# Weight units of a two-block kernel loaded by two transfers (120 and 8 partitions) instead of one of 128

## The chip, the cores and the metric

The program runs on one core of one Trainium2 chip. The metric is the time of one execution on the device in microseconds (us), of which the median over several runs is compared.

## The reference, cut to what matters

The input is a sequence of 512 tokens of width 1024 in float32. It passes through two blocks.

The first block normalises the tokens, multiplies them by a weight matrix `w_in`, and takes from the product the inputs of a convolution branch, of a windowed attention branch with 16 heads, and of two sets of gates. The branches are projected, gated, added, projected again by `w_out`, and added to the input. After that comes a feed-forward part over 16,384 experts. A query projection gives scores; for each of the 512 tokens and each of 8 heads the 16 best experts are picked, and the rows of `peer_u` and `peer_v` that belong to them are read:

```python
u = expert_u[expert_idx]
act = gelu(einsum('thkd,td->thk', u, hc))
vv = expert_v[expert_idx]
return einsum('thk,thkd->td', gate * act, vv)
```

These are 512 x 8 x 16 pairs of rows of 2 x 1024 numbers each, 536.9 MB.

The second block normalises again, multiplies by a second `w_in`, and runs three branches (a recurrence over the tokens, a sliding-window attention, a cross attention to a memory of 256 tokens), which are gated, projected and added.

## The kernel before, in words

**Weight units.** All projection weights are laid out on the host as 171 units. One unit is 128 partitions x 1024 float32 numbers, 512 KB, so 4 KB for each partition. They lie in the order of their use: 28 for the first product, 24 that fill other stages, 16 for merging, 16 for the queries of the experts, 8 for the memory, and 79 for the second block. The class `Weights` handles them:

- `load` (L198, on SyncE's queue, SP) sends unit u into slot u % 4 of a ring of four (`weight_ring`). Before it, L197 waits until unit u - 4, which lay in that slot, has been used up (`done`). When the transfer has landed, the semaphore `arrived` of the slot has gone up by 16.
- `high_part` (L206, on ScalarE, ACT) waits for `arrived` and rounds the unit into `weight_high`. It is called by `finished`, which waits until unit u is done and then takes unit u + 2.
- `low_parts` (L223) or `low_part` (L231), on GpSimd (POOL) or for the first units on VectorE (DVE), subtract the rounded part from the unit and write the rest over it.
- TensorE (PE) multiplies with three products for each tile (L155 to L157): high x high, high x low, low x high. The last of a unit's 24 matmuls raises `done`.

So the load of unit u + 4 is issued when unit u is done, and its rounding starts when unit u + 2 is done: a load has the time of two units.

**What else is on SyncE's queue.** It works in order. In most stages `load` calls alternate with stores of finished tiles to HBM (`z_store`, L303), with reads of them (`merge_z`, L951 and L2802), and, in the experts' stage, with stores of the scores (`score_store`, L1180) and their reads (`peer_sc`, L1175). At the start SyncE issues x and the constants (L825) and then the first four units.

**The experts' stage.** GpSimd issues 512 indirect gathers (L1349). Each reads one expert for each of 128 tokens, 1 MB in rows of 8 KB, into one of ten slots of `peer_uv`. VectorE multiplies and sums the first half of each row with the token (L1548), ScalarE applies gelu (L1309) and builds diagonal matrices (L1314), and TensorE adds the second halves with them (L1655). The last matmul of two gathers frees their slots. The last units of the query weights and the eight of the memory are loaded, rounded and used beside the gathers; the loads stand at L1178 and L1191.

Of the kernel before, what the change touches and what calls it, by code (L numbers as in the profile page):

```python
# [27 lines left out]
P = 128  # L28
# [7 lines left out]
RING = 4  # L36
# [46 lines left out]
def offsets(widths):  # L83
    at, out = 0, {}
    for name, w in widths.items():
        out[name] = (at, at + w)
        at += w
    return out, at


class Columns:


    def __init__(self, tensor, widths):
        self.tensor, (self.at, self.width) = tensor, offsets(widths)
# [36 lines left out]
def placed(nc, ctx, name, shape):  # L132

    tensor = ctx.enter_context(nc.sbuf_tensor(name, shape, F32))
    return tensor, nc.sbuf_base - 4 * int(np.prod(shape[1:]))


def same_place(nc, name, shape, offset):


    return nc.alloc_sbuf_tensor_at(name, shape, F32, offset=offset)
# [18 lines left out]
class Weights:  # L160
# [2 lines left out]

    def __init__(self, nc, ctx, dram):
        self.nc, self.dram = nc, dram
        self.ring, offset = placed(nc, ctx, "weight_ring", [P, RING, DT, P])
        self.low = same_place(nc, "weight_low", [P, RING, DT, P], offset)
        self.high, self.high_offset = placed(nc, ctx, "weight_high", [P, 2, DT, P])  # L170
        self.arrived = [ctx.enter_context(nc.semaphore(f"weights_arrived{s}")) for s in range(RING)]
        self.high_ready = ctx.enter_context(nc.semaphore("weights_high_ready"))
        self.split = ctx.enter_context(nc.semaphore("weights_split"))
        self.done = ctx.enter_context(nc.semaphore("unit_done"))
        self.issued = self.highs = self.lows = 0
# [15 lines left out]
    def load(self, sp, upto):  # L191

        upto = max(min(upto, TOTAL), self.issued)

        def one(u, i):
            if u >= RING:
                sp.wait_ge(self.done, RING * i + (u - RING + 1))  # L197
            sp.dma_start(self.ring[:, u % RING], self.dram[u + RING * i]).then_inc(self.arrived[u % RING], 16)  # L198
        self.units(sp, self.issued, upto, one)
        self.issued = upto  # L200

    def high_part(self, act, u, i=0):

        if u < TOTAL:
            act.wait_ge(self.arrived[u % RING], 16 * i + 16 * (u // RING + 1))
            self.nc.scalar.activation(self.high[:, u % 2].bitcast(F32R), self.ring[:, u % RING], ACT.Copy  # L206
                                      ).then_inc(self.high_ready, 1)
            self.highs = u + 1
# [2804 lines left out]
```

## Time and profile before

| | us |
|---|---|
| median of 3 runs | 2619.27 (2618.55 to 2622.28) |
| the profiled execution, its own time | 2615.85 |
| its span, first to last instruction | 2614.0 |
| around the span | 1.85 |
| TensorE busy | 2224.1 (85%) |
| VectorE busy | 1661.2 (64%) |
| ScalarE busy | 872.3 (33%) |
| GpSimd busy | 853.1 (33%) |
| mean rate of the 16 DMA engines | 261 GB/s |

The profile is of one execution. It cuts the span into 40 equal slices of 65.35 us; a digit is the busy share of an engine in that slice, in tenths. The shares are averages over stages that have different limits, so each stage has to be read by itself.

### The profile page before, as it was taken

Reading aid. Unit: us, or ns where it says so; the run is one execution under the profiler, and the core shown is the slowest. Engines: PE = TensorE matmul, PEld = TensorE weight load, DVE = VectorE, ACT = ScalarE, POOL = GpSimd, SP = SyncE. Lnnn points to the kernel's source line nnn. Section 1 sums busy time; section 2 is a strip of 40 time slices with the busy share of each in tenths; the row PEclk is TensorE's granted clock in tenths of the full one; section 3 lists DMA queues with packets and bytes.
Section 4 is the critical chain, followed back from the end, with each engine's and each line's share of the span. In section 5 each row is a group of like instructions: output and inputs, shape, how many; then the busy total and the mean of one; then the engine's idle time right before and its main releaser. Section 6 shows DMA issues by size and latency. Waiting matters only on the chain. (4 is left out here: it accounts for less than half of the span.)

```text
span 2614.0 us, 33173 instructions
## 1 busy us (share of the span) xinstructions
PE 2224.1 (85%) x11846; PEld 1388.6 (53%) x11846; DVE 1661.2 (64%) x3847; ACT 872.3 (33%) x1939; POOL 853.1 (33%) x649
## 2 busy tenths in 40 slices
PE   8998999889987888777777777777788999989999
PEld 7886667765543333322222222322266788766787
DVE  7998797257776777766776667766403533546443
ACT  3222762333323242322322223222233322235531
POOL 0001213355443455444433343333232212112243
PEclk9999999999999999999999999999989999979999
DMA  4332215289999999999999999999722222332253
GB/s 152 105 109 85 84 51 177 73 301 419 421 422 419 421 420 419 420 418 416 416 420 416 417 407 420 413 415 416 312 89 74 73 71 68 104 113 86 89 189 105
DMA packets 131073, 682.46 MB, mean 261 GB/s; under 512 B 13536, under 2 KB 23136, under 8 KB 65120
## 3 DMA queue, kind: packets, MB, share of 16 engines
q0 software_dynamic: 73728, 536.90, 49.7%
q1 hardware_dynamic: 57184, 143.47, 16.0%
q8 instruction: 94, 1.54, 0.2%
q14 instruction: 67, 0.55, 0.1%
HBM read 655.68 MB, written 24.64 MB: 260 GB/s over the span
## 5 line engine op out<-in xcount | busy, mean ns | idle before, releaser
L1655 PE MATMUL bank<-peer_uv,peer_diag 128*128 128x512 f32 x2048 | 959.6, 613 | 299.2 <-ACT peer_diag L1314 292.4
L1548 DVE SCALAR_TENSOR_TENSOR peer_uv<-peer_uv,early_h 128x1024 f32<-128x1024 f32 x512 | 639.5, 1260 | 389.4 <-DMA peer_uv<-in_peer_uv,peer_index 389.4
L1655 PEld LDWEIGHTS bank<-peer_uv,peer_diag 128*128 128x128 f32 x2048 | 379.3, 194 | 841.4 <-issue 838.4
L1349 POOL DMA_INDIRECT peer_uv<-in_peer_uv,peer_index x512 | 524.0, 1024 | 753.6 <-PE bank L1655 665.0
L223 POOL TENSOR_TENSOR weight_low<-weight_ring,weight_high 128x1024 fp32r<-128x1024 f32 x102 | 249.0, 2442 | 703.5 <-ACT weight_high L206 703.5
L155 PE MATMUL bank<-hT_high,weight_high 128*128 128x512 f32 x952 | 404.3, 425 | 16.9 <-PEq L1675 3.9
L157 PE MATMUL bank<-hT_high,weight_low 128*128 128x512 f32 x952 | 375.4, 394 | 0.0
L156 PE MATMUL bank<-hT_low,weight_high 128*128 128x512 f32 x952 | 375.1, 394 | 0.0
L206 ACT ACTIVATE weight_high<-weight_ring 128x1024 fp32r<-128x1024 f32 x171 | 180.7, 1057 | 468.3 <-PE bank L157 448.1
L1309 ACT ACTIVATE peer_gelu<-peer_dots 128x2 f32<-128x2 f32 x256 | 52.1, 203 | 801.9 <-DVE peer_uv L1548 801.9
L155 PEld LDWEIGHTS bank<-hT_high,weight_high 128*128 128x128 f32 x952 | 182.0, 191 | 72.7 <-issue 20.8
L1314 ACT ACTIVATE peer_diag<-const,peer_weight 128x128 f32<-128x128 f32 x512 | 177.5, 393 | 114.6 <-DVE peer_weight L1453 109.6
L156 PEld LDWEIGHTS bank<-hT_low,weight_high 128*128 128x128 f32 x952 | 181.9, 191 | 44.1 <-issue 10.7
L157 PEld LDWEIGHTS bank<-hT_high,weight_low 128*128 128x128 f32 x952 | 181.0, 190 | 39.5
L231 POOL TENSOR_TENSOR weight_low<-weight_ring,weight_high 128x1024 fp32r<-128x1024 f32 x29 | 79.5, 2743 | 291.5 <-ACT weight_high L206 291.1
L868 DVE SCALAR_TENSOR_TENSOR convT_whole<-z_u,cols,convT_whole 128x512 f32<-128x512 f32 x120 | 89.2, 743 | 0.0
L868 DVE SCALAR_TENSOR_TENSOR z_odd<-z_u,cols,z_odd 128x512 f32<-128x512 f32 x112 | 83.2, 743 | 0.0
L1453 DVE SCALAR_TENSOR_TENSOR peer_weight<-peer_gelu,peer_r,peer_e 128x2 f32<-128x2 f32 x256 | 54.5, 213 | 39.7 <-ACT peer_gelu L1309 39.7
L470 DVE SCALAR_TENSOR_TENSOR attn_logit<-const,bank 128x256 f32<-128x256 f32 (+2 forms) x96 | 39.2, 449 | 44.8 <-PE bank L415 44.5
L494 DVE TENSOR_SCALAR attn_prob<-attn_prob,attn_recip 128x256 f32<-128x256 f32 (+2 forms) x112 | 63.0, 598 | 0.1
L231 DVE TENSOR_TENSOR weight_low<-weight_ring,weight_high 128x1024 fp32r<-128x1024 f32 x40 | 48.7, 1217 | 10.1 <-ACT weight_high L206 10.1
L1309 ACT ACT_TABLE_LOAD x40 | 51.3, 1283 | 0.7
(410 smaller groups left out, 2696.8 us busy)
## 6 DMA issues: line engine op xcount, KB each, us to landing
weight_ring<-in_weights SPq DMA_DIRECT2D x171, 512.0 KB, 3.7
z_store<-fill_stage SPq DMA_DIRECT2D x70, 256.0 KB, 2.4
peer_uv<-in_peer_uv,peer_index POOLq DMA_INDIRECT x512
merge_z<-z_store SPq DMA_DIRECT2D x8, 768.0 KB, 6.2
merge_z<-z_store SPq DMA_DIRECT2D x12, 512.0 KB, 5.0
score_store<-peer_work SPq DMA_DIRECT2D x16, 192.0 KB, 11.6
peer_sc<-score_store SPq DMA_DIRECT2D x24, 128.0 KB
swz<-z_store SPq DMA_DIRECT2D x1, 2560.0 KB, 11.2
```

Of the source, the lines that this page charges most:

```text
L155: nc.tensor.matmul(to, left[0], right[0], start=start, stop=False)
L156: nc.tensor.matmul(to, left[0], right[1], start=False, stop=False)
L157: return nc.tensor.matmul(to, left[1], right[0], start=False, stop=stop)
L206: self.nc.scalar.activation(self.high[:, u % 2].bitcast(F32R), self.ring[:, u % RING], ACT.Copy).then_inc(self.high_ready, 1)
L223: self.nc.gpsimd.tensor_tensor(self.low[:, slot].bitcast(F32R), self.ring[:, slot], self.high[:, u % 2], ALU.subtract).then_inc(self.split, 1)
L231: vector.tensor_tensor(self.low[:, u % RING].bitcast(F32R), self.ring[:, u % RING], self.high[:, u % 2], ALU.subtract).then_inc(self.split, 1)
L868: nc.vector.scalar_tensor_tensor(to, u[:, c, k:k + T], cols("conv_w", k * DT + c), to, ALU.mult, ALU.add).then_inc(tap_done, 1)
L1309: nc.scalar.activation(gelu[:, at], dots[:, at], ACT.Gelu).then_inc(gelu_done, 1)
L1314: nc.scalar.activation(diag[:, p % SLOTS], ident, ACT.Copy, scale=weight[:, p % TOPK:p % TOPK + 1]).then_inc(diag_ready, 1)
L1349: pool.indirect_dma_start(uv[:, p % SLOTS], None, peer_uv, bass.IndirectOffsetOnAxis(index[:, n % 2, p % TOPK:p % TOPK + 1], 0)).then_inc( ...
L1548: nc.vector.scalar_tensor_tensor(uv[:, p % SLOTS, 0:D], uv[:, p % SLOTS, 0:D], 1.0, h2[:, t], ALU.mult, ALU.mult, accum_out=dots[:, p % TO ...
L1655: mm = nc.tensor.matmul(bank[2 * (t % 2) + c][:], diag[:, p % SLOTS], uv[:, p % SLOTS, D + c * 512:D + (c + 1) * 512], start=(p % PICKS == ...
```

## The change

Each unit is sent by two transfers on the same queue, one after the other: partitions 0 to 119, then 120 to 127. Each of them raises the slot's semaphore by 16, so the waiting side counts in steps of 32. Bytes, slots, order, and all other instructions are the same.

```diff
+    MOST = 120
...
         def one(u, i):
             if u >= RING:
                 sp.wait_ge(self.done, RING * i + (u - RING + 1))
-            sp.dma_start(self.ring[:, u % RING], self.dram[u + RING * i]).then_inc(self.arrived[u % RING], 16)
+            for rows in (slice(0, self.MOST), slice(self.MOST, P)):
+                sp.dma_start(self.ring[rows, u % RING], self.dram[u + RING * i][rows]).then_inc(self.arrived[u % RING], 16)
...
         if u < TOTAL:
-            act.wait_ge(self.arrived[u % RING], 16 * i + 16 * (u // RING + 1))
+            act.wait_ge(self.arrived[u % RING], 32 * i + 32 * (u // RING + 1))
```

## Rows read from the trace of the kernel before

**Rows 1.** The page's 40 slices: busy tenths by engine, DMA share, GB/s.

```profile
PE   8998999889987888777777777777788999989999
DVE  7998797257776777766776667766403533546443
DMA  4332215289999999999999999999722222332253
GB/s 152 105 109 85 84 51 177 73 301 419 421 422 419 421 420 419 420 418 416 416 420 416 417 407 420 413 415 416 312 89 74 73 71 68 104 113 86 89 189 105
```

**Rows 2.** Stretches: engine busy us (instructions), granted TensorE clock, DMA share, GB/s.

```profile
440.00:500.00 60.00, 56.83 (x244) 45.41 (x242) 22.92 (x33) 16.87 (x23) 24.55 (x10) 1.00 0.30 99
...
1200.00:1400.00 200.00, 149.17 (x326) 59.34 (x326) 139.16 (x383) 59.00 (x155) 79.83 (x79) 0.98 1.01 417
```

**Rows 3.** Waits over the whole span, us in total, times, longest.

```profile
POOL peer_uv L1349 <- PE bank L1655: 665.0, 244, 6.5
...
DVE peer_uv L1548 <- DMA peer_uv<-in_peer_uv,peer_index: 389.4, 235, 9.7
...
ACT weight_high L206 <- DMA weight_ring<-in_weights: 11.9, 2, 8.0
```

**Rows 4.** All 171 loads (L198): SyncE's issue time in ns, and us to landing.

```profile
L198 SPq DMA_DIRECT2D weight_ring<-in_weights x171: 327/332/992, 3.6 to 2587.5; - x171
...
DMA to landing us min/median/max: 3.4/3.7/15.6
```

**Rows 5.** ScalarE's timeline while units follow each other: start, us, instruction, idle before.

```profile
440.87 1.06 ACT L206 ACTIVATE weight_high<-weight_ring 128x1024 fp32r<-128x1024 f32 x1 [4.54 <-PE bank L157]
446.47 1.06 ACT L206 ACTIVATE weight_high<-weight_ring 128x1024 fp32r<-128x1024 f32 x1 [4.54 <-PE bank L157]
```

**Rows 6.** The waits of SyncE's own queue.

```profile
SPq L198 <- PE bank L157: 952.4, 147, 97.9
```

**Rows 7.** ScalarE's timeline where the gathers begin.

```profile
558.35 1.06 ACT L206 ACTIVATE weight_high<-weight_ring 128x1024 fp32r<-128x1024 f32 x1 [8.02 <-DMA weight_ring<-in_weights]
...
564.46 1.06 ACT L206 ACTIVATE weight_high<-weight_ring 128x1024 fp32r<-128x1024 f32 x1 [3.91 <-DMA weight_ring<-in_weights]
...
567.96 0.20 ACT L1309 ACTIVATE peer_gelu<-peer_dots 128x2 f32<-128x2 f32 x1
```

**Rows 8.** The loads issued beside the gathers, from 560 us on.

```profile
L198 SPq DMA_DIRECT2D weight_ring<-in_weights x18: 327/458/496, 560.8 to 1058.0; - x18
...
DMA to landing us min/median/max: 5.2/9.1/15.5
```

**Rows 9.** DMA queues by packets, MB and share of 16 engines, 1200 to 1400 us.

```profile
q0 software_dynamic: 11348, 82.65, 100.1%
```

**Rows 10.** The same, 106 to 109.6 us: one load lands alone.

```profile
DMA packets 144, 0.52 MB, mean 146 GB/s; under 512 B 16, under 2 KB 16, under 8 KB 144
...
q1 hardware_dynamic: 144, 0.52, 44.6%
```

**Rows 11.** Three stretches of 20 us in which the gathers run below their rate (columns as in rows 2).

```profile
1540.00:1560.00 20.00, 15.54 (x35) 5.93 (x33) 14.06 (x42) 6.26 (x15) 8.19 (x8) 1.00 0.98 384
1240.00:1260.00 20.00, 16.14 (x32) 6.42 (x32) 13.92 (x38) 3.79 (x13) 8.80 (x9) 0.91 1.00 405
1640.00:1660.00 20.00, 15.47 (x32) 6.05 (x31) 13.45 (x35) 5.11 (x18) 8.66 (x8) 0.91 1.00 400
```

**Rows 12.** The first load, issued at 3.56 us.

```profile
DMA to landing us min/median/max: 8.3/8.3/8.3
```

**Rows 13.** ScalarE's timeline where it takes the first unit.

```profile
12.50 0.20 ACT L767 ACTIVATE z_rms<-z_ms 128x1 f32<-128x1 f32 x1 [1.08 <-DVE z_ms L837]
12.61 1.04 ACT L206 ACTIVATE weight_high<-weight_ring 128x1024 fp32r<-128x1024 f32 x1
```

## Prediction

> **What bounds the kernel now.** I read the slices first, since this kernel has stages with different limits [rows 1]. From about 560 to 1880 us the DMA digit is 9 and the rate stands at 413 to 422 GB/s in nearly all slices, while TensorE falls to 7 or 8 and VectorE to 6 or 7. Before and after that TensorE is at 8 or 9 and the DMA engines at 1 to 5. So there are two regimes, and the change, which touches only DMA transfers, has to be priced in each.
>
> Then come two stretches [rows 2]. In the first TensorE is busy 56.83 of 60 us and the DMA share is 0.30: TensorE is the bound. In the second TensorE is busy 149 of 200 us and the DMA share is 1.01: the gathers are the bound. The waits say the same [rows 3]. VectorE waited 389.4 us for gathered rows, in 235 places. GpSimd's wait of 665.0 us for TensorE is for free slots; it costs nothing as long as the engines have gathers queued, and a share of 1.0 says that they have.
>
> The weight loads themselves stand in the list of waits once: ScalarE waited for a load twice, 11.9 us together [rows 3]. All other 169 found their unit landed.
>
> **The change, part by part.**
>
> *Issue on SyncE.* There are 171 more DMA instructions. One takes a median of 0.33 us [rows 4], up to 0.49 beside the gathers [rows 8], so SyncE is occupied for some 57 to 84 us more. None of it should reach the end: at the loads SyncE sits waiting for TensorE for 952.4 us, in 147 of the 171 cases [rows 6]. What stands behind a load in this queue (the tile stores, the reads for merging, the score stores) is delayed by 0.33 to 0.49 us each. Nobody waits for a tile store; the readers prefetch two tiles ahead. I cost this at nothing. Its cover is that slack; without it the cost would be 0.33 us for each of some 40 loads that a read or a score store follows, 13 us.
>
> *Landing in the TensorE stages.* A load lands 3.7 us after issue [rows 4]. Units follow each other in 5.60 us (446.47 - 440.87, [rows 5]), and a load has two units, 11.2 us. 7.5 us are spare. The second issue adds 0.33 us, and one more packet on some engine about 0.2 us: 128 packets of 4 KB took 44.6% of 16 x 3.6 us, 0.20 us each [rows 10]. Even if all 8 rows of the small transfer went through one engine, 8 x 0.20 = 1.6 us would fit. About 150 of the loads lie there: cost 0. The first unit lands at 3.56 + 8.3 = 11.9 us [rows 12] and is taken at 12.61, with no wait on the load, right behind the step at 12.50 [rows 13]. One packet more still fits into these 0.7 us: 0.
>
> *Bytes beside the gathers.* Here the engines have no idle time, so every microsecond that a load takes from the busiest engine is paid. Eighteen loads are issued from 560 us on [rows 8], and the one for which ScalarE waits until 564.46 [rows 7] was issued before them: 19. The packets of a gather give the price: 82.65 MB in 100.1% of 16 x 200 us is 0.0388 us per KB, so 0.16 us for a row of 4 KB and 0.32 for one of 8 KB [rows 9]. Before, one transfer is 128 packets of 4 KB and 16 small ones [rows 10], which I read as eight rows for each of 16 engines and an end mark from each. After, 120 rows can't be even (7.5 each), and 8 rows are sent apart. The trace of before shows no such transfer, so I bound it. Low end: the busiest engine still carries 8 rows, 0 us. High end: the busiest ones carry 16, 8 x 0.16 x 19 = 24 us. I take 9 rows, the full eight of the large transfer plus one of the small, since eight is what each engine carries today: 19 x 0.16 = **3.0 us**.
>
> By the Trainium skill, "DMA: Bandwidth & Descriptors", section "Why a DMA increments its semaphore by 16 and not by 1", a transfer uses the largest number of engines up to 16 that divides its rows, from the lowest-numbered on: 15 for 120 rows, 8 for 8. Eight engines would carry nine rows, seven eight and one none, and by that the sum would be the same 3.0 us; no row here shows it.
>
> *The handover to the gathers.* The two loads for which ScalarE waits end at 558.35 and 564.46 us; gelu of the first gathers starts only behind them, at 567.96 [rows 7]. Between two packets of a load an engine sends one of a gather, so one row more comes 0.16 + 0.32 = 0.5 us later. The second wait ends by its own load, so the two don't add: **0.5 us**, with 0 and 3.8 us (eight rows) as ends.
>
> *Given back.* A lag of a few engines is lost again where the gathers run below their rate for another reason. Against 421 GB/s, three stretches of 20 us miss (1 - 384/421) x 20 = 1.8, 0.8 and 1.0 us [rows 11], and all come after the last load at 1058 us. There the engines that aren't behind idle a little longer and the others catch up. They need not be the same waits; I take **-1 us**, with 0 and -3.5 as ends.
>
> The sum is 3.0 + 0.5 - 1.0 = **+2.5 us**. On the profiled execution that is a span of 2616.5 and a time of 2618.4 us. It lay 3.4 us below the median of the runs, so against the median of 2619.3 I forecast **2621.8 us**. That is +0.1%, less than the 0.2% (5.2 us) that a measurement of this kernel can tell from no change.
>
> **The rivals.**
>
> *A. Wholly hidden, 2619 us.* The busiest engine gets no more than today, or the lag is all caught up in the dips. For it: some 3.6 us of dips [rows 11] can cover 3.5. Against it: they are short, and a share of 0.98 to 1.00 in them means that most engines are still busy.
>
> *B. Slower by over 0.2%: the gathers lose more than a row per load.* The place is the stretch from the handover to 1066 us, where 19 loads share saturated engines. If each costs r packets of 4 KB instead of one, because its rows are divided unevenly or because two engines then write to the same part of SBUF and hold each other up, the price is r x 3.0 + 0.5 us. From r = 2 it passes 5.2 us. At r = 4, half of the eight rows, it is +12.5, 2631.8 us; at r = 8, with 3.8 us at the handover, +27.8, 2647 us. For it: a gather's pace is that of the slowest engine, and these stages have no spare share [rows 2]. Against it: ten gathers are in flight, so engines can take turns in lagging.
>
> By the Trainium skill, "SBUF — State Buffer", section "Door 1: The DMA port swizzle", four neighbouring partitions share a port, the next four lie on another, and 32 further it is the same port again. If the 15 engines take eight neighbouring rows each, engine and port no longer match one to one as in the transfer of 128; that is the second cause in B. No row here shows ports.
>
> *C. Faster: one engine paces the gathers, and it is relieved.* If one engine that is slower than the rest gets no row of the loads any more, it saves up to 8 x 0.16 x 19 = 24 us, but no more than its distance from the next slowest. Against it: an engine that all others wait for would leave them idle, and the share is 1.01 [rows 2], 100.1% for the gathers' queue alone [rows 9]. What is left is under 1% of 500 us, 5 us; I give it -6 us, 2613. The Trainium skill, "DMA: Bandwidth & Descriptors", section "Latency and other measured facts", says that engines 7 and 15 are usually slower in traces, which is what would make this case; it names two, and relieving one of them leaves the other.
>
> *D. The large transfer uses only a few engines.* With one engine it would take 120 x 0.2 = 24 us, over twice the 11.2 us that it has; the TensorE stages would be bound by it, some 13 us for each of 150 units, a time over 4000 us. Nothing in the trace points to it, and nothing excludes it but that 120 divides well.
>
> **How the numbers follow.** Forecast 0.47, A 0.20, B 0.26, C 0.06, D 0.01. The forecast's own bounds run from +0 to about +6 us: with the scatter of the median I put 0.05 of its 0.47 above +5.2. Faster by over 0.2%: C, 0.06. Slower: B, D and that 0.05, 0.32. Within: 0.62. The range must leave out 0.2 at most: the lower end takes in A and most of C with the 0.1% scatter of the runs, 2614; the upper end takes in B up to r = 4 or 5, 2634. Outside are r above 5, D and the rest of C, together some 0.17.
>
> **What would show each step right or wrong.** The small packets of a load, 16 now, tell how many engines it uses: 23 would be 15 and 8. The loads become 342 issues, with SyncE's medians near 0.33 us, and TensorE's busy time stays near 2224 us. The landing of the loads in the quiet stages stays below 5 us; over 11 us would be D. ScalarE's waits for loads stay two, near 8.5 and 4 us; a third means that cover is gone. The step between the handover and the end of the gathers, 560 to 1893 us, grows by 2 to 3 us, all of it before 1066 us (the last load's issue and landing); growth by 6 or more there is B, and packets of the weight loads then take clearly more than 0.16 us each. A stretch that shrinks there is C. Growth anywhere else proves the forecast wrong in its first two steps.

## The result and the profile after

| | before | after |
|---|---|---|
| median us | 2618.91 | 2655.99 |
| range of four runs | 2615.91 to 2622.28 | 2652.69 to 2659.00 |
| profiled execution, own time | 2615.85 | 2656.61 |
| its span | 2614.0 | 2654.8 |

The change makes the kernel slower by 37.1 us: the ratio is 1.0151, with a 95% interval of 1.0139 to 1.0163. The forecast was +2.5 us and the range ended at 2634. Both were wrong.

The DMA share and the rate of after in 40 slices, against [rows 1] (a slice is 66.4 us now):

```profile
DMA  5433316289999999999999999999922222332373
GB/s 150 107 104 83 84 53 179 75 299 391 384 390 412 420 377 379 390 414 415 421 415 418 420 413 416 411 419 415 384 76 75 83 58 69 91 124 84 87 193 105
```

The DMA digit is 9 in the experts' stage as before. The rate is not as before: 391, 384 and 390 GB/s in three slices, then 412 and 420, then 377, 379 and 390, and from there on 411 to 421 until the slice in which the gathers end. The two valleys are where weight units are loaded, eight in each (before, they were issued from 596 to 760 us and from 905 to 1058 us). Between and after them the gathers run at the rate of before.

Stretches of after (engine busy us and instructions, granted clock, DMA share, GB/s):

```profile
600.00:800.00 200.00, 175.28 (x523) 93.53 (x521) 137.61 (x326) 58.69 (x151) 95.06 (x78) 0.97 1.02 386
800.00:930.00 130.00, 95.68 (x225) 39.87 (x224) 89.50 (x242) 39.69 (x103) 49.31 (x50) 0.99 1.02 420
930.00:1100.00 170.00, 138.33 (x323) 64.73 (x321) 104.07 (x283) 54.55 (x128) 77.73 (x64) 0.89 1.01 382
1200.00:1400.00 200.00, 154.97 (x322) 62.02 (x323) 138.51 (x383) 59.51 (x157) 80.84 (x78) 0.94 1.01 417
```

and the same of before:

```profile
600.00:800.00 200.00, 179.43 (x526) 94.22 (x525) 142.84 (x344) 63.77 (x163) 97.66 (x83) 0.99 1.02 421
800.00:905.00 105.00, 81.97 (x193) 34.38 (x192) 76.54 (x210) 32.59 (x87) 41.28 (x41) 0.98 1.01 421
905.00:1066.00 161.00, 134.22 (x333) 62.72 (x331) 112.89 (x291) 57.52 (x139) 83.08 (x68) 0.96 1.02 419
```

Beside the loads the rate fell from 421 to 386 and from 419 to 382, (1 - 386/421) x 200 = 16.6 and (1 - 382/419) x 170 = 15.0 us. The DMA share stayed 1.01 to 1.02. Behind the loads it was 417 again, as in [rows 2]. So the engines were as busy as before and moved less: a busy share of 1 says that packets are in flight, not that they are fast.

The first and the last gather on GpSimd's timeline, before and then after:

```profile
540.07 1.09 POOL L1349 DMA_INDIRECT peer_uv<-in_peer_uv,peer_index  x1 [2.70 <-DVE peer_index L1435]
1870.30 0.94 POOL L1349 DMA_INDIRECT peer_uv<-in_peer_uv,peer_index  x1 [0.30 <-issue]
```

```profile
543.26 1.09 POOL L1352 DMA_INDIRECT peer_uv<-in_peer_uv,peer_index  x1 [2.71 <-DVE peer_index L1438]
1911.26 0.94 POOL L1352 DMA_INDIRECT peer_uv<-in_peer_uv,peer_index  x1 [0.30 <-issue]
```

Of the 40.8 us between the two spans, 3.2 are there before the first gather, 37.8 come between the first and the last (40.96 - 3.19), and nothing is added behind. What precedes the gathers was expected to be free. It starts with ScalarE taking the first unit late, against [rows 13]:

```profile
13.79 1.06 ACT L209 ACTIVATE weight_high<-weight_ring 128x1024 fp32r<-128x1024 f32 x1 [0.59 <-DMA weight_ring<-in_weights]
```

That is 1.2 us: 0.5 were there one instruction earlier (`z_rms` starts at 13.00 instead of 12.50), and 0.59 are a wait for the load. Most of the rest comes between 240 and 300 us, where the granted clock of TensorE was 0.89 in this profile and 0.94 in that of before: GpSimd's first `weight_low` starts at 238.2 instead of 237.5 us, and the one at 292.5 starts at 295.6. The first experiments below show whether these 3.2 us belong to the change.

The handover, against [rows 7]:

```profile
562.40 1.06 ACT L209 ACTIVATE weight_high<-weight_ring 128x1024 fp32r<-128x1024 f32 x1 [8.88 <-PE bank L157]
...
571.89 1.06 ACT L209 ACTIVATE weight_high<-weight_ring 128x1024 fp32r<-128x1024 f32 x1 [7.30 <-DMA weight_ring<-in_weights]
```

The second unit is taken 571.89 - 564.46 = 7.4 us later, of which 3.2 were there already: the handover cost 4.2 us.

Last, the loads alone. One load in a window of 5 us without gathers, DMA queues by packets, MB and share of 16 engines, before:

```profile
DMA packets 144, 0.52 MB, mean 105 GB/s; under 512 B 16, under 2 KB 16, under 8 KB 144
...
q1 hardware_dynamic: 144, 0.52, 32.1%
```

and after:

```profile
DMA packets 151, 0.52 MB, mean 105 GB/s; under 512 B 23, under 2 KB 23, under 8 KB 151
...
q1 hardware_dynamic: 151, 0.52, 39.5%
```

The 23 small packets, one end mark for each engine by the prediction's reading, fit 15 and 8 engines. That agrees with the rule in the Trainium skill, "DMA: Bandwidth & Descriptors", section "Why a DMA increments its semaphore by 16 and not by 1"; the count alone doesn't exclude another pair with this sum. The share tells more: the same 128 rows occupy engines for 0.395 x 16 x 5 = 31.6 us instead of 25.7, with nothing else beside them. Single loads scatter: for the one in 95 to 100 us it is 36.8% against 33.7%, 29.4 against 27.0 us. Over all loads before the gathers, 0 to 530 us, the difference is clear. SyncE's queue before, after, and for three other ways of sending a unit that the experiments below introduce (112 + 16 partitions, 64 + 64 partitions, two halves of the columns):

```profile
q1 hardware_dynamic: 19008, 54.96, 30.5%
q1 hardware_dynamic: 19503, 54.93, 37.3%
q1 hardware_dynamic: 20192, 54.96, 33.2%
q1 hardware_dynamic: 20165, 54.92, 38.5%
q1 hardware_dynamic: 29664, 54.96, 30.4%
```

The bytes are the same within 0.1% and the packets differ only by end marks, but in the last line by twice the packets as well, and there the share doesn't rise. So it isn't the number of packets or of transfers that makes packets last longer, but the split by partitions, even without gathers.

### The profile page after: what moved, and what is told of

It reads as the page before. It is cut to its first block and busy times, and to the rows that moved or that the text cites. A ratio compares the mean times of both kernels' runs of the same rounds, so it can differ in the third digit from the quotient of the medians.

```text
span 2654.8 us, 33384 instructions
## 1 busy us (share of the span) xinstructions
PE 2241.7 (84%) x11846; PEld 1395.2 (53%) x11846; DVE 1654.9 (62%) x3847; ACT 872.6 (33%) x1939; POOL 853.5 (32%) x649
## 3 DMA queue, kind: packets, MB, share of 16 engines
q1 hardware_dynamic: 58381, 143.48, 18.9%
## 5 line engine op out<-in xcount | busy, mean ns | idle before, releaser
L1658 PE MATMUL bank<-peer_uv,peer_diag 128*128 128x512 f32 x2048 | 976.1, 622 | 319.6 <-ACT peer_diag L1317 310.1
L1658 PEld LDWEIGHTS bank<-peer_uv,peer_diag 128*128 128x128 f32 x2048 | 385.9, 197 | 870.9 <-issue 868.2
L1456 DVE SCALAR_TENSOR_TENSOR peer_weight<-peer_gelu,peer_r,peer_e 128x2 f32<-128x2 f32 x256 | 56.4, 220 | 41.8 <-ACT peer_gelu L1312 41.8
```

The costliest lines, as they stand in the source:

```text
L1658: mm = nc.tensor.matmul(bank[2 * (t % 2) + c][:], diag[:, p % SLOTS], uv[:, p % SLOTS, D + c * 512:D + (c + 1) * 512], start=(p % PICKS == ...
```

## The experiments

Three theories were set against each other. **U**: the cost comes from uneven engines (nine, eight or no rows). **N**: it comes from having two transfers. **P** (place): it comes from which partitions each engine writes, since engines that write to the same part of SBUF at the same time slow each other.

All kernels below differ from before only in a list of pieces that `load` sends one after the other; the waiting side counts the pieces of each slot.

```diff
-            sp.dma_start(self.ring[:, u % RING], self.dram[u + RING * i]).then_inc(self.arrived[u % RING], 16)
+            for to, of in self.pieces(u):
+                sp.dma_start(to(self.ring[:, u % RING]), of(self.dram[u + RING * i])).then_inc(self.arrived[u % RING], 16)
```

"Beside the gathers" means the 20 units `first_unit("query") + 8 <= u < first_unit("query") + 28`: the last eight of the queries, the eight of the memory and the first four of the second block.

**Where the cost lies.** First 120 + 8 for the 20 units beside the gathers only:

```diff
+        cuts = (120, 8) if first_unit("query") + 8 <= u < first_unit("query") + 28 else (128,)
```

> Only the 20 units whose loads are issued from 542 us on, beside the gathers, are sent as 120 + 8 partitions; the other 151 go as one transfer. The cost lies beside the gathers (all theories on how it comes about): +33 to +36 us on before, ratio 1.013, of the +37 of the whole change. If it is the number of transfers on SyncE's queue in general: 20/171 of it, +4 us, 1.002.

Measured: 2653.66 us against 2615.45, +38.2 us, ratio 1.0149 (1.0132 to 1.0166), 2 us above the expected range and in agreement with the +37.1 of the whole change. Then the complement, 151 units split and these 20 whole:

> The complement of the last one: 151 units as 120 + 8, the 20 beside the gathers as one transfer. Cost beside the gathers: only the shifts at the start (+1.2 us) and around 250 us (+2.4) stay, +3 to +4 us, ratio 1.001 to 1.002. If every load costs: +33 us.

Measured: 2615.86 us, +0.4 us, ratio 1.0006 (0.9996 to 1.0015). The whole cost is in the 20 units, 1.9 us for each. The 151 others are free within what can be measured. The expected +3 to +4 us didn't come, so the 3.2 us ahead of the gathers in the profile of after aren't a sure part of the result. The profile of this kernel, which splits the same loads there, also shows ScalarE waiting for the first unit (0.51 us), but its granted clock from 240 to 300 us is 0.94 as before, and its first gather starts at 540.60 us, 0.5 later than before. With columns halved, a kernel that comes below, the clock there is 0.89 again and the first gather starts at 542.05.

**Uneven, two, or place.** An even split in two, by intent 7 rows and 1 row for each engine:

```diff
+        cuts = (112, 16)
```

> All units as 112 + 16 partitions: 7 rows and 1 row for each of 16 engines, 8 rows on each as before, 32 end marks per load. Theory U, uneven load of the engines (nine, eight and no rows): the cost goes, under +5 us, below 1.002. Theory P, place: an engine's rows are no longer those of one part of SBUF that it has to itself, and engines hold each other up; evenness doesn't help: +25 to +45 us, 1.010 to 1.017, and 4 KB packets of the loads take 0.20 us or more beside the gathers. Theory N, two transfers instead of one: as the change, +37 us, with packets at 0.16 us.

Measured: 2644.90 us, +29.5 us, ratio 1.0111 (1.0095 to 1.0128). From 600 to 750 us, 4 KB on SyncE's queue, its other transfers included, took 0.209 us of an engine (10.3% of 16 x 150 us for 4.85 MB), and 0.176 before (9.4% for 5.26): P's sign as well. And an even split in halves:

```diff
+        cuts = (64, 64)
```

> All units as 64 + 64 partitions, 4 rows per engine and transfer, even. U: below 1.002. N: +37 us, 1.014. P: sixteen engines write into one half of SBUF at a time, so they hold each other up at least as much as with 120 + 8: +30 to +60 us, 1.011 to 1.023.

Measured: 2654.55 us, +39.1 us, ratio 1.0149 (1.0132 to 1.0166). Both programs have 59,920 packets on SyncE's queue against 57,184, 16 more for each of 171 loads, which fits 16 end marks for each of the two transfers. U falls with these two: where all 16 engines take part in both transfers and the rows divide evenly, 29 and 39 us are lost. N is still open, and goes with the next, two transfers of all 128 partitions and half the columns each:

```diff
+        return [((lambda t, e=e: t[:, 4 * e:4 * e + 4]), (lambda t, e=e: t[:, 512 * e:512 * e + 512])) for e in range(2)]
```

> All units as two transfers of 128 partitions each, 512 columns (2 KB per row) in each. As many transfers as in the change, but every engine keeps the rows of the single transfer. Theory P (place): the cost goes; only 128 packets more per load, whose 2 KB take 0.084 us instead of 0.080, 0 to +4 us, 1.000 to 1.0015. Theory N (two transfers instead of one): +37 us, 1.014.

Measured: 2618.74 us against 2615.59, +3.2 us, ratio 1.0010 (1.0000 to 1.0019). As many transfers, and twice the packets for each load, cost 3 us, between 0 and 5 by the interval. The rates in 40 slices of the 150 us from 600 on show it best. Before, six loads land here and can't be seen:

```profile
GB/s 425 412 427 419 422 428 417 421 419 427 419 419 417 421 428 419 422 421 411 424 430 424 419 415 425 414 420 431 419 419 426 414 423 430 415 415 419 420 427 417
```

With 120 + 8 each is a hole of two or three slices of 3.75 us:

```profile
GB/s 406 398 281 324 377 422 419 422 425 419 329 289 422 419 422 417 423 338 294 425 422 414 419 362 283 401 422 419 418 419 409 294 345 419 419 424 417 354 280 409
```

With halves of the columns there are none:

```profile
GB/s 417 410 423 424 422 421 421 420 424 412 419 420 421 418 419 418 424 422 417 421 422 418 420 417 419 416 426 425 410 424 422 418 419 424 420 413 417 426 420 415
```

**Place alone.** A pair of kernels that differ in nothing but the place. Both send partitions 64 to 127 of the 20 units in one transfer and 0 to 63 in eight transfers of eight partitions. In the one they are neighbours:

```diff
+        at = [slice(8 * m, 8 * m + 8) for m in range(8)] + [slice(64, P)]
```

> Only the 20 units beside the gathers: partitions 0 to 63 by eight transfers of eight neighbouring partitions, 64 to 127 by one transfer. The busiest engines carry 12 rows: U alone gives +4 x 0.16 x 20 = +13 us. P: the eight engines of a small transfer write next to each other and take turns, up to 4 rows one after the other: 0.48 us lost for each of 8 x 20 small transfers, +77 us, with the large one's +20 and the unevenness +60 to +110 us, 1.023 to 1.042.

Measured: 2692.73 us, +77.1 us, ratio 1.0294 (1.0277 to 1.0311). In the other each transfer takes every fourth partition of 32:

```diff
+        at = [slice(32 * h + a, 32 * h + 32, 4) for h in range(2) for a in range(4)] + [slice(64, P)]
```

> The same with partitions 0 to 63 by eight transfers of every fourth partition, so that engine j gets the rows of the four-partition group that it has in the single transfer too. Same number of transfers, same bytes and rows per engine as with neighbouring partitions; only the place differs. P: +15 to +35 us (half of 64 + 64's loss, and the unevenness), at least 30 us less than with neighbours. U and N: the same time as with neighbours within 5 us.

Measured: 2654.65 us, +39.1 us, ratio 1.0147 (1.0130 to 1.0164). The same transfers, bytes and packets: both programs have 58,464 packets on SyncE's queue, 64 more than before for each of 20 loads, which is eight end marks for each small transfer. Neighbours cost 38.1 us more, 0.24 us for each of 160 small transfers. The +39 of the spread one is above the +35 that was given as its highest value: half of 64 + 64's loss (20) and the unevenness (13) make 33, and 6 us are unexplained. The DMA queues of the two, 600 to 750 us, neighbours first:

```profile
q0 software_dynamic: 6941, 50.56, 90.9%
q1 hardware_dynamic: 3597, 4.38, 9.8%
```

```profile
q0 software_dynamic: 7190, 52.35, 90.6%
q1 hardware_dynamic: 3792, 4.85, 10.1%
```

The gathers' queue (q0) holds the engines for the same share in both, and moves 50.56 against 52.35 MB in it. It moved 57.80 before. The gathers' own packets slow down; it isn't only that the loads take longer.

This pair changes the place in SBUF and in HBM at once. The next two part them. In the first the small transfers write neighbouring partitions (`NEAR`, the first list of slices) and read every fourth row (`FAR`, the second), in the other the reverse:

```diff
-        return [((lambda t, s=s: t[s]), (lambda t, s=s: t[s])) for s in at]
+        return [((lambda t, s=s: t[s]), (lambda t, r=r: t[r])) for s, r in zip(NEAR, FAR)]
```

> The pair of eights changed two places at once: where the rows lie in SBUF and where in HBM. Here the small transfers write eight neighbouring partitions and read every fourth row of HBM; so the weights of these 20 units come in a wrong order of rows, and the output is another. If the place in SBUF is what counts: the time with neighbours, +72 to +82 us, 1.0275 to 1.0315. If the place in HBM counts: the time with spread rows, +34 to +44 us, 1.013 to 1.017.

> The reverse: the small transfers read eight neighbouring rows of HBM and write every fourth partition (again the rows of these 20 units in a wrong order). SBUF counts: +34 to +44 us, 1.013 to 1.017. HBM counts: +72 to +82 us.

Measured: neighbours in SBUF 2692.09 us against 2617.04, +75.1 us, ratio 1.0288 (1.0271 to 1.0305); neighbours in HBM 2657.87 us, +40.8 us, ratio 1.0163 (1.0144 to 1.0182). The time follows the place in SBUF, not that in HBM; the difference of 34.2 us is 0.21 us for each of 160 small transfers. This is P by itself. With wrong weights these two kernels may gather other experts, but behind the loads, from 1200 to 1400 us, both move 414 GB/s (417 before), so that isn't what sets them apart.

**How it grows.** The 20 units as four transfers of 32 neighbours (two rows per engine), and as eight of 16 (one row per engine):

```diff
+        at = [slice(32 * m, 32 * m + 32) for m in range(4)]
```

> Only the 20 units beside the gathers, as four transfers of 32 neighbouring partitions: two rows for each of 16 engines, so two engines share each group of four partitions, as they share a part of SBUF with 64 + 64. P: about the loss of 64 + 64, +30 to +45 us, 1.011 to 1.017. U: 0, since every engine still carries eight rows.

```diff
+        at = [slice(16 * m, 16 * m + 16) for m in range(8)]
```

> The same as eight transfers of 16 neighbouring partitions: one row for each of 16 engines, four engines on each group of four partitions, the same crowding as with eight neighbouring partitions, where neighbours cost 38 us more than spread rows, 0.24 us for each of 160 transfers. P: 0.24 to 0.48 us for each of 160, and more than with 32 neighbours: +45 to +80 us, 1.017 to 1.031. U: 0.

Measured: 2653.72 us against 2616.02, +37.7 us, ratio 1.0142 (1.0125 to 1.0159), and 2675.75 us, +59.7 us, ratio 1.0226 (1.0209 to 1.0243). Their packets (58,144 and 59,424) fit 16 end marks for each transfer in both, and so rows that divide evenly, eight for each engine. With 64 or 32 neighbours in a transfer the loss is the same 38 to 39 us; with 16 neighbours, four engines on four partitions, it is half as large again.

## Why the prediction was wrong, step by step

**Issue on SyncE: right.** 171 issues more, median 0.32 us, and SyncE still sat waiting for TensorE 147 times:

```profile
L201 SPq DMA_DIRECT2D weight_ring<-in_weights x342: 272/324/864, 3.6 to 2628.6; - x171
```

```profile
SPq L201 <- PE bank L157: 936.4, 147, 97.8
```

**Landing in the TensorE stages: right in the time, with one reading wrong.** 151 split units cost +0.4 us, within the interval of nothing. But "One packet more still fits into these 0.7 us: 0" did not hold: ScalarE waited 0.59 us for the first unit, and 0.51 in the kernel with 151 split units, where it didn't reach the end. ScalarE's waits for loads stayed two, but not the same two: one at the start, one of 7.30 us at the handover, while the unit before that one now shows a wait for TensorE.

**Bytes beside the gathers: this is the step that failed.** It priced a load by the packets on the busiest engine, each at the 0.16 us that packets take from the gathers' rate, "19 x 0.16 = 3.0 us". The number of end marks was as assumed, but the price of a packet was not a constant. What the split adds is not one packet; it makes all of them slower, those of the gathers too. From 600 to 750 us, 4 KB of the gathers took 0.169 us of an engine instead of 0.157 (91.0% of 16 x 150 us for 52.88 MB, against 92.1% for 57.80), and 4 KB on SyncE's queue 0.215 instead of 0.176 (10.6% for 4.85 MB, against 9.4% for 5.26). In the timeline of the gathers, the ninth starts 7.4 us later than before (575.52 against 568.08) and the 201st, behind the last load, 41.8 us (1120.43 against 1078.59): the term measured 34.4 us, 1.8 us for each of 19 loads, eleven times what I took. (The load issued at 542.6 us, before, took 15.6 us to land and lies beside the gathers too, so there are 20; that changes little.) It even lies above the bound that I gave as the high end, "8 x 0.16 x 19 = 24 us". That bound held only if the engines are the narrowest part: it counted rows on an engine and left out that the rate also depends on which places in SBUF are written at the same time, as the pairs at +77.1 against +39.1 us and at +75.1 against +40.8 show.

A sum that gives about the 37 us can be put together from the experiments afterwards, as an estimate: 29.5 us as with 112 + 16, 20 x 0.24 = 4.8 us for the small transfer of eight neighbours, and the 3.0 us for the ninth row, 37.3 in all. No run shows that these parts add up. The last of them was never run alone, since every uneven split that I found also changes the place; how much is unevenness stays open.

**The handover: right in kind, too small.** "0.5 us, with 0 and 3.8 us (eight rows) as ends" measured 4.2 us in the profile. It belongs to the same loads: less what the first gather was late, the second unit was taken 2.8 us later than before with only the 20 units split, and 0.8 us earlier with only the 151 split. That the reason is the same slowdown is likely and not shown by itself.

**Given back: right in size, by luck as far as the runs show.** The 41.8 us behind the last load are 41.0 at the last gather; 0.9 us came back where I took "-1 us". From the 201st gather to the last it took 790.8 us after, 791.7 before, and 790.9 with only the 20 units split, but 791.7 with every fourth partition, where as much had been lost, and 793.2 with neighbours. So the profiles scatter by as much as the term. With 3.2 us ahead of the gathers and 4.2 at the handover the profiled execution comes out: 3.2 + 4.2 + 34.4 - 0.9 = 40.9.

**The rivals.** B came true in its second cause: "two engines then write to the same part of SBUF and hold each other up". It had a chance of 0.26, but its price was put in multiples of one row and its likeliest at r = 4; it was r = 12. Of its signs, growth beside the gathers by 6 us or more came, and so did the slower packets. What spoke against it, ten gathers in flight, did not prevent the loss; my reading, not shown, is that it can't where the place is the narrow part, since all ten write there. The Trainium skill, "SBUF — State Buffer", section "Door 1: The DMA port swizzle", makes four neighbouring partitions share a port; the two pairs of eights agree, +77.1 and +75.1 us with neighbours in SBUF, +39.1 and +40.8 with every fourth. By the Trainium skill, "DMA: Bandwidth & Descriptors", section "The descriptor swizzle", a transfer of 128 partitions gives each engine rows of one port that no other engine of the transfer writes. No trace here shows ports or engine numbers, but only the kernels that keep 128 partitions in a transfer ran at full rate. C would have shown a faster stretch and did not. A needs a load that costs nothing beside the gathers; 1.9 us each is the opposite. D is excluded by the 23 small packets and by the TensorE stages, which lost nothing.

The profile of before could have warned in one way: in the experts' stage 16 engines moved 421 GB/s with a share of 1.02. It didn't say whether engines or memory set that, and I took the engines without a row that excludes the other.

## What to carry to other kernels

When a transfer is split by partitions, its bytes and engines can stay the same and its cost still change: keep all 128 partitions in each piece and cut along the free dimension, where that is needed (+3 us here against +29 to +77). What a DMA costs in a stage bound by DMA is read from the rate in GB/s, not from the busy share, which stayed at 1.02 while 8% of the rate went. In the stages bound by TensorE the split cost nothing that could be measured (+0.4 us for 151 loads). And a price per packet from an undisturbed pattern holds only for transfers of that pattern; its bound must hold another shared part as well.

## What the runs showed of the hardware that was not expected

- A load of 512 KB beside the gathers, sent as 120 and 8 partitions, costs 1.9 us more than when sent whole, more than the 1.25 us that its bytes take at 421 GB/s.
- Small transfers whose rows are neighbouring partitions are slower than those with every fourth partition: 0.24 us for each of eight rows and eight end marks, at equal bytes and packets (0.21 in the crossed pair), and only where the rows are neighbours in SBUF. With 16 rows a transfer the loss was 3.0 us per load, with 32 or 64 rows 1.9 to 2.0.
- The slowdown needs no gathers: before they start, from 0 to 530 us, the packets of SyncE's queue held the engines for 37.3% instead of 30.5%, and for 30.4% with two halves of the columns. In the TensorE stages this is hidden.
- A load sent as 120 and 8 rows had 23 small packets, which fits 15 and 8; over the whole program 58,381 packets of the queue against 57,184, seven more for each of 171 loads.
